# Causal mask from bf16 tables and values' products of two heads per bank in the prompt attention of a hybrid decoder kernel

## The reference, cut to what matters

```python
s = jnp.einsum('bqhc,bkc->bhqk', q_lat, c) + jnp.einsum('bqhr,bkr->bhqk', q_rope, kr)
s = s.astype(jnp.float32) * MLA_SCALE
s = jnp.where(k_pos[None, None, None, :] <= q_pos[None, None, :, None], s, -jnp.inf)
pr = jax.nn.softmax(s, axis=-1).astype(c.dtype)
...
o = jnp.einsum('bhqk,bkc->bqhc', pr, c)
```

## Time and profile before

| | us |
|---|---|
| median of 3 runs | 861.76 |
| the three runs | 861.78, 861.76, 857.13 |
| span of the profiled execution, first to last instruction | 859.9 |
| TensorE busy in it | 796.4 |
| stage of the second row tile, from the first scores to the last values' product | 499.7 to 586.6 |

### The profile page before, as it was taken

The page is one execution under the profiler, slowest core; times in us unless marked ns, Lnnn a source line. Parts: engine busy times, 40 slices in busy tenths (PEclk is TensorE's granted clock), DMA queues, the critical chain, the costliest instruction groups (busy, mean ns, idle before and its releaser), DMA issues.

```text
span 859.9 us, 20149 instructions
## 1 busy us (share of the span) xinstructions
PE 796.4 (93%) x8431; PEld 565.8 (66%) x8431; DVE 372.6 (43%) x819; ACT 278.1 (32%) x592; POOL 171.6 (20%) x221
## 2 busy tenths in 40 slices
PE   8989989999999999999979989989999989999791
PEld 6778777767555547878865677768766767655440
DVE  4994322756423222045842353333644466342232
ACT  4433353041131342155444322231670061132232
POOL 8000780001011000000039933003700001011000
PEclk9999999999899999999999877996999999999997
DMA  9935902764999999332010140003726665999982
GB/s 241 325 115 94 213 14 95 289 267 166 415 415 414 416 369 251 112 121 77 1 19 5 33 144 15 3 3 87 224 72 228 262 246 199 416 417 415 416 343 75
DMA packets 73440, 172.65 MB, mean 201 GB/s; under 512 B 11851, under 2 KB 50178, under 8 KB 64284
## 3 DMA queue, kind: packets, MB, share of 16 engines
q1 hardware_dynamic: 64548, 149.81, 48.5%
q0 software_dynamic: 8576, 20.86, 7.4%
q10 hardware_dynamic: 224, 0.67, 0.8%
HBM read 161.54 MB, written 9.66 MB: 199 GB/s over the span
## 4 chain that ended last, share of the span: by engine, by line
PE 75%; DVE 9%; DMA 6%; issue 4%; ACT 4%; SPq 0%; POOLq 0%; DVEq 0%; ACTq 0%
PE bank L1825 15%; PE bank L2282 9%; PE bank L2149 7%; PE bank L2329 5%; DVE scratch L2422 4%; PE bank L873 3%; DMA scratch<-in_moe_w_gate 3%; PE bank L1785 3%; DMA scratch<-in_moe_w_up 3%; PE bank L2339 2%; PE bank L705 2%; PE bank L1002 2%; PE bank L2390 1%; DVE scratch L2425 1%; PE bank L2271 1%
## 5 line engine op out<-in xcount | busy, mean ns | idle before, releaser
L2941 ACT ACTIVATE scratch<-bank 128x512 f32<-128x512 f32 (+8 forms) x108 | 51.6, 495 | 346.6 <-PE bank L2329 134.5
L1825 PE MATMUL bank<-x_fm,weight_slots 128*128 128x280 f32 x576 | 140.5, 403 | 3.4 <-issue 2.7
L1825 PEld LDWEIGHTS bank<-x_fm,weight_slots 128*128 128x128 f32 x576 | 109.6, 192 | 30.4 <-issue 4.3
L2282 PE MATMUL bank<-weight_slots,scratch 128*64 128x256 f32 x576 | 87.7, 383 | 0.0
L2282 PE MATMUL bank<-scratch 128*64 128x256 f32 x448 | 73.1, 384 | 3.8 <-DMA scratch<-in_moe_w_gate 2.5
L2282 PEld LDWEIGHTS bank<-weight_slots,scratch 128*64 128x64 f32 x576 | 54.3, 138 | 29.7 <-issue 7.5
L1616 POOL DMA_INDIRECT scratch<-x_rows_dram,row_of_slot x14 | 13.4, 958 | 246.9 <-DVE row_of_slot L2739 169.4
L2149 PE MATMUL bank<-scratch,weight_slots 128*128 128x280 f32 x256 | 62.5, 402 | 0.0
L2149 PEld LDWEIGHTS bank<-scratch,weight_slots 128*128 128x128 f32 x256 | 48.1, 190 | 13.3 <-issue 1.3
L2282 PEld LDWEIGHTS bank<-scratch 128*64 128x64 f32 x448 | 46.3, 139 | 15.8 <-DMA scratch<-in_moe_w_gate 3.3
L2422 DVE TENSOR_TENSOR scratch<-scratch 128x128 f32<-128x128 f32 (+13 forms) x68 | 44.5, 673 | 26.3 <-ACT scratch L2941 24.7
(11 more groups left out here) (514 smaller groups left out, 1321.0 us busy)
## 6 DMA issues: line engine op xcount, KB each, us to landing
weight_slots<-in_moe_w_gate SPq DMA_DIRECT2D x24, 1024.0 KB, 17.7
scratch<-in_moe_w_up SPq DMA_DIRECT2D x20, 1024.0 KB, 12.4
scratch<-in_moe_w_down SPq DMA_DIRECT2D x20, 1024.0 KB, 13.2
weight_slots<-in_moe_w_down SPq DMA_DIRECT2D x12, 1024.0 KB
weight_slots<-in_moe_w_up SPq DMA_DIRECT2D x12, 1024.0 KB, 17.1
weight_slots<-in_od_w_in SPq DMA_DIRECT2D x9, 1024.0 KB, 8.9
weight_slots<-in_ev_w_in SPq DMA_DIRECT2D x8, 1024.0 KB, 12.9
scratch<-in_moe_w_gate SPq DMA_DIRECT2D x8, 1024.0 KB
```

The costliest lines, as they stand in the source:

```text
L1825: ins = pe.matmul(b[:, 0:NT], w[:, k, P * m2:P * m2 + P], src[:, k, :], start=(k == 0), stop=(k == kt - 1))
L2282: ins = pe.matmul(b[CAP * j:CAP * j + CAP, 0:DE], XG[:, q % 2, k, CAP * j:CAP * j + CAP], w[j][:, k, :], start=(k == 0), stop=(k == KD - 1))
L2941: return act.activation(dst, b[:rows, 0:width], f, **kw).then_inc(ring.free, 1)
```

## The change

The mask's product takes bf16 copies of the identity and of the causal table, which DVE makes once at the start of the second mixer, in the place of the table `cosd`. The values' products of two heads go to the lower and upper 64 partitions of one bank, alternating product by product, at part 1 of every even head from 2 to 8; `PTS` gets two buffers, and one copy takes the bank of both heads.

```diff
         Q96, VM, K96, SCM, CT9 = flat(0, MH, NT), flat(2240, 3, 512), flat(4096, MH, NT), flat(6336, 2, 3, NPR), flat(11360, 3, 288)
         PTO = [0, 272, 416]
-        PTS = part(24700, 432)
+        PTS = part(24700, 2, 432)
+        at = COFF["cosd"][0]
+        IDB, CAUB = (CST[:, at + 64 * i:at + 64 * i + 64].bitcast(BF16) for i in range(2))
...
                     pe.matmul(to, Q96[0:96, h, c0:c0 + r], K96[0:96, h, 0:c0 + r], start=True, stop=False)
-                    ins = pe.matmul(to[:, c0:c0 + r], ident[:r, 0:r], cst("causal")[:r, 0:r], start=False, stop=True)
+                    ins = pe.matmul(to[:, c0:c0 + r], IDB[:r, 0:r], CAUB[:r, 0:r], start=False, stop=True)
...
             def attend(h):
 
                 until("vm")
-                until(f"pts{h}")
+                until(f"pts{h + 1}")
                 b = W.claim()
-                o = 64 * (h % 2)
                 for j, (j0, rj) in enumerate(PT):
-                    ins = pe.matmul(b[o:o + 64, j0:NPR], VM[:rj, j, VH * h:VH * h + VH], PTS[:rj, PTO[j]:PTO[j] + NPR - j0], start=(j == 0), stop=(j == 2))
+                    for i in range(2):
+                        ins = pe.matmul(b[64 * i:64 * i + 64, j0:NPR], VM[:rj, j, VH * (h + i):VH * (h + i) + VH], PTS[:rj, i, PTO[j]:PTO[j] + NPR - j0], start=(j == 0), stop=(j == 2))
                 close(W, ins, f"yd{h}")
...
                     if part_ == 0 and h < MH:
                         scores(h)
-                    if part_ == 1 and 0 < h <= MH:
-                        attend(h - 1)
+                    if part_ == 1 and 0 < h <= MH and h % 2 == 0:
+                        attend(h - 2)
...
         def odd_dve(dve, V, s, until, empty, mul, add, sub, centre, scale, out_and_moe):
+            s.mark(dve.tensor_copy(IDB, ident), dve_step)
+            s.do(dve.tensor_copy(CAUB, cst("causal")))
             until("od16")
...
             def probs_turned(h):
 
                 b = W.take()
-                act.activation(PTS[:, 0:416], b[:, 0:416], ACT.Copy)
-                act.activation(PTS[0:16, 416:432], b[0:16, 416:432], ACT.Copy).then_inc(w_free, 1)
+                act.activation(PTS[:, h % 2, 0:416], b[:, 0:416], ACT.Copy)
+                act.activation(PTS[0:16, h % 2, 416:432], b[0:16, 416:432], ACT.Copy).then_inc(w_free, 1)
 
             def attend(h):
 
                 b = W.take()
-                o = 64 * (h % 2)
-                act.activation(MIXS1[o:o + 64, h // 2, 0:NPR], b[o:o + 64, 0:NPR], ACT.Copy).then_inc(w_free, 1)
+                act.activation(MIXS1[:, h // 2, 0:NPR], b[:, 0:NPR], ACT.Copy).then_inc(w_free, 1)
...
-                    if part_ == 1 and 0 < h <= MH:
-                        attend(h - 1)
+                    if part_ == 1 and 0 < h <= MH and h % 2 == 0:
+                        attend(h - 2)
```

## The result

The changed kernel is slower: 868.43 us against 862.1 us in the median of 20 runs each, and the ratio is 1.0084 (95% interval 1.006 to 1.0108). Measured again beside other kernels it was 1.0086 (1.0045 to 1.0127). The forecast was 857.1 in a range of 851.5 to 865.5, so the time lies outside the range as well.

A forecast was written before the change was run, and what follows sets the result against it. TensorE was taken to bound the stage, with a second chain through DVE and ACT beside it from head 3's next round; 3.2 us (mask) plus 1.45 (values' products) off gave 857.1 us, range 851.5 to 865.5.

The forecast's parts named there:

- The mask's product: Attention scores on TensorE: bf16 mask products save 0.36 us a head, 3.2 us in all.
- rival B: Mask's product: changing between f32 and bf16 drains TensorE, the mask gives nothing, only 1.45 us remain; 860.3 us, chance 0.13.
- The table copies: Start of the second mixer: two DVE copies of 128 x 128 fall in idle time and cost nothing.
- The pair takes what one head takes: Values' products of two heads on TensorE: column halves run side by side, a pair takes 1.06 to 1.1 us.
- Heads 3 and 7, nothing gained: Values' products taken out there gain 0: head 3 waits for DVE's division, head 7's fillers wait longer for ACT.
- Head 5, 0.95 us gained: Values' product taken out at head 5: all of it is gained, as line 934 follows on TensorE; 0.95 us.
- the next thing late is line 934 itself: Head 5: DVE's division comes behind line 934 and is not late, so the block's 0.95 us is saved.
- Head 1, 0.5 us gained: Values' product taken out at head 1: between 0 and 1.06 us, as an earlier start need not hasten instruction supply; 0.5 taken.
- All four blocks together: Values' products taken out at heads 1, 3, 5 and 7: 1.45 us gained together, between 0 and 4.2.
- The sum: Whole kernel: 3.2 us from the mask plus 1.45 from the values' products, 4.7 us less; 857.1 us, chance 0.50.
- Rival C: Heads 3 onward: without the values' product, stops come sooner among small products and the clock falls; chance 0.22.
- C's price: Half clock taking heads 3 and 4 too: 7.5 us more, 864.6 us; with heads 3 to 6, 14 more, 871.

The follow-up runs named there:

- e2: Kernel before with only the mask's product changed to bf16, table copies included: 861.4 us, ratio 0.9995 to the kernel before.
- e10: Kernel before with only the mask's product changed to bf16, measured again: 857.9 us, ratio 0.9952 to the kernel before.
- e3: Changed kernel with the f32 mask and no table copies, so only the pairs of values' products: 870.8 us, ratio 1.0043 to the kernel before.
- e5: Changed kernel with two filler products where each odd head's values' product stood, same kernel as e4 measured again: 857.4 us, ratio 0.9974 to the kernel before.
- e8: Kernel before without its own two filler products ahead of the turned probabilities of seven heads: 869.0 us, ratio 1.0112 to the kernel before.
- e4: Changed kernel with two filler products of 256 columns where each odd head's values' product stood: 856.7 us, ratio 0.9889 to the kernel before.
- e11: Changed kernel with the f32 mask, no table copies, and the fillers of e4: 854.7 us, ratio 0.9948 to the kernel before.

## Why the prediction was wrong

**The mask's product: right.** 0.15 us was taken for 128 columns and 0.15 was measured; 0.36 us a head, measured 0.37; 3.2 us in all, measured 3.5 at equal half clock (e2, e10). The changes between f32 and bf16 ate nothing of this that shows, so rival B falls.

**The table copies: right.** In the changed kernel's profile they take 0.28 and 0.22 us from 346.4, with DVE idle behind them until 358.84, and nothing waits for them.

**The pair takes what one head takes: right,** 1.08 us.

**Heads 3 and 7, nothing gained: right in the chain, wrong in the effect.** At head 7 the fillers were to wait longer for ACT; they wait for nothing now, and the wait stands behind them, 1.69 us for the division. At head 3 the predicted wait of about a us was filled by the stop of 1.54 us in this execution, and the clock fell with it.

**Head 5, 0.95 us gained: wrong.** The step "the next thing late is line 934 itself" overlooked that this line claims all four banks of its ring and so waits until DVE has read the one of line 921 before it. The values' product had covered just that: where it stood, TensorE waits 0.95 us, and from line 921 to that line it is 2.04 us as before. The gain is nil.

**Head 1, 0.5 us gained: about nil in the balance.** The stop is longer where TensorE comes to it earlier, as I allowed for: 0.89 us in the profile before, 1.11 and 1.94 in the two of the changed kernel. That it grows for this reason is not shown, since the two executions of one kernel lie further apart than that. All four blocks together were put at 1.45 us; e3 gives 0.1 ± 1.9 at equal half clock.

**The sum failed at the clock.** This is the step that failed: the sum has no term for the clock, it carried the half clock of the kernel before over unchanged. Rival C had the direction (the products out, rounds of small products in a row, a stop, the clock falls) and a chance of 0.22. That the stop is what makes the clock fall is not shown: behind e5's stops of 1.10 and 0.83 us it held, in e10 it fell behind one of 0.38. C's price, one added stretch of 7.5 us to a time of 864.6, was too small by 4 us; the far end that I gave it, 871, is 3 us too high. Measured: 23 to 30 us more half clock in a run, at 0.34 us each 8 to 10 us, against 3 us of work saved. The reason that I gave against C, that the same rounds passed at the full clock at head 3, was worthless, since in that profile the values' product still stood between them. And what I had in front of me I read as a cost only: fillers that make no result, put by hand where TensorE waits, speak of a stage that needs work there to keep its clock, as e8 shows.

## What to carry to other kernels

Where TensorE's clock is at its edge (a stage of small products whose windows show both levels in one profile), count wide work that is taken out as a possible loss, and ask what it covered: here a wait for DVE, and the clock. Put a filler of the same width into the hole, at the very place, and the saving elsewhere stays: with fillers, e4 and e11 are faster than both kernels of this case, by 1.1 and 0.5% against the one before, and so is the mask alone in e10, by 0.5% (the intervals of e5, the same kernel as e4, and of e2, the same as e10, reach no change). Which of these versions is the best the runs don't settle. Compare such kernels over many runs and at equal half clock; one pair of profiles shows mostly where the stretches happened to fall.

## What was not expected of the hardware

TensorE's stops with nothing waited for stand at a fixed count of its instructions: 64 instructions more ahead of one moved it by 32 product records, from 180 to 148, and edits that took instructions out left the count at 10,290. Other stops stand near 9,784, 10,795, 11,300 and 12,313 in several profiles each, so 505 or 506 apart, or twice that. That they are loads of program code is the likely reading (the page's instruction queue moved 68 packets, 1.11 MB, 16 KB each), but the transfers were not changed in any run. They lasted 0.4 to 2 us and fell among the small products. And a filler pays: seven pairs of products without a result were worth 1.1% of the kernel (e8).
